# Memory tokens and memory K/V weights ahead of the first modulation weights, their products among them and out of the block attention

## The chip, the core and the metric

The kernel runs on one core of one Trainium2 chip. The metric is the device time of one execution in microseconds, the median of the runs shown. TensorE (PE in the profile) multiplies into eight PSUM banks of 128 x 512 fp32; VectorE (DVE) and ScalarE (ACT) read these and work in SBUF; GpSimd (POOL) builds masks at the start; SyncE (SP) issues nearly all loads, from one queue.

## The reference

Two blocks, one after the other, on 256 tokens of 1024 channels, in fp32. The first computes modulation vectors, a mixer of two halves (a recurrence and causal attention), and a mixture of 32 experts; the second is a stick-breaking attention with an attention on 256 memory tokens, and a feed-forward layer.

```python
# first block
mods = silu(c) @ w_ada + b_ada                      # shift1, scale1, gate1, shift2, scale2, gate2
h = rms_norm(x, norm1_g) * (1 + scale1) + shift1
proj = h @ w_in
y_rwkv = rwkv7_time_mix(proj[..., :RWKV_PROJ], ...)
y_moba = moba_attention(proj[..., RWKV_PROJ:], ...)
x = x + gate1 * (concat(y_rwkv, y_moba) @ w_out)
h = rms_norm(x, norm2_g) * (1 + scale2) + shift2
x = x + gate2 * moe_ffn(h, ...)                     # top 4 of 32 experts
# second block
proj = x @ w_in_sb;  mix = stick_breaking_attention(q, k, v)
mem_out = memory_attention(q_mem, mem, w_mem_kv)    # keys and values: mem @ w_mem_kv
x = layer_norm(ALPHA * x + concat(mix, mem_out) @ w_out, ...)
x = layer_norm(ALPHA * x + square(relu(x @ w_up)) @ w_down, ...)
```

`mem @ w_mem_kv` depends on inputs alone, on nothing that the first block computes. Its result (km, the keys with channels on partitions, and vmem, the values with tokens on partitions) is wanted in the second block only.

## The kernel before

All instructions are written out by hand in one program for each engine; the order in the code is the order on the engine, and semaphores tie the engines. Weights pass through `ring`, ten slots of 2 MB. During the first block's mixer the slots 4 to 7 serve as work space (`ws`), and the slots 0 to 3 take the weights of the prologue, in the order of the list `PRO` (22 entries, `pro_slot(n)`): four pieces of the modulation weights `w_ada` (2 MB each, the first 2048 columns, 256 rows a piece), then the seven pieces of `w_in`, with further pieces of `w_ada` between them, then the memory weights, and the rest. A slot is loaded again when `pro_freed(n)` says that its piece is used, which TensorE counts in `halves_used` and VectorE in `mod_acc`.

**Front.** SyncE loads x, then the first four pieces of `w_ada`. The memory tokens are loaded before entry 4, once the first piece is used. TensorE turns the rows of small parameters (L614, a helper for all transposes), turns x (16 transposes 128 x 128), sums the squares (L628), and multiplies silu(c) with the four pieces (L642, 32 matmuls; a matmul of fp32 gives two records in the profile where its row says so, so that a piece has 8 matmuls and 16 records). The result is copied (L1528), turned, and makes shift and scale; then the memory tokens are turned (four groups, `mem_turned`) and VectorE copies them to `memT` (L1896). ScalarE (L1534) and VectorE (L1892) write the modulated input hT, and the projections start (`proj`, L685).

**Middle.** Projections, the preparation of the recurrence, and the block attention, in which four pairs of heads follow each other (`for i in range(RT)` on PE). Per pair: scores (L758, L759), VectorE adds the position term and takes the maxima (`moba_max`, L2003 to L2009), ScalarE takes exponentials with their sums (`moba_exp`, L1626), VectorE divides (`moba_norm`, L2015 to L2018), TensorE turns the probabilities (6 transposes, L614), issues the scores of the pair after next and one of four parts of the memory product (`mem_kv_part`, L809 for the two halves of km, L812 for those of vmem: 8 matmuls each), ScalarE copies the turned probabilities (L1635, L1636), TensorE multiplies with the values (L851, L853), and ScalarE copies the output (L1640) and, after every second pair, km or vmem from bank 6 (L1643). Then comes the recurrence (`wkv_setup` from L864 on), which waits for the last output copy, the last copy of turned probabilities, and vmem. ScalarE's order in this loop is: copies of pair i, exponentials of pair i + 2, output copy of pair i.

**Experts.** The first loads of expert weights wait for the milestone `y_ready` at the end of the recurrence (the four slots of `ws`), the next for the slots of `w_out`. 32 passes follow, each with six loads of 2 MB, and then the second block.

The waits that the change touches are these:

```python
if n == 4:
    load(mem_tok, a["mem_2"]..., S("mem_in"))          # SP
if job == 1:
    pe.wait_ge(S("memT_ready"), 4)                     # PE, in proj
if i == 2:
    pe.wait_ge(S("mem_kv"), 1)                         # PE, in mem_kv_part
pe.wait_ge(S("mem_kv"), 2)                             # PE, before wkv_setup
```

Of the kernel before, what the change touches and what calls it, by code (L numbers as in the profile page):

```python
# [17 lines left out]
ACT = mybir.ActivationFunctionType  # L18
# [32 lines left out]
N_PRO = 22  # L51
# [54 lines left out]
def build(nc, a, out):  # L106
    ctx = ExitStack()
    with ctx:
# [176 lines left out]
        memT = view(tok_f, 0, [KT, T])  # L285
# [47 lines left out]
        def chunk_cols(w, c0, n):  # L333
# [8 lines left out]
               + [("mem", 0), ("ada", 9), ("out", 0), ("out", 1), ("ada", 10), ("ada", 11)])  # L342
# [14 lines left out]
        def pro_slot(n):  # L357
            return (n + 2) % PRO_RING
# [24 lines left out]
        def _(sp_):  # L383
# [9 lines left out]

            load(tok[:, :, :], a["x"][0].rearrange("(i p) d -> p i d", p=P), S("x_in"))
            for n in range(N_PRO):
# [4 lines left out]
                if n == 4:  # L400
                    load(mem_tok, a["mem_2"][0].rearrange("(i p) d -> p i d", p=P), S("mem_in"))
# [8 lines left out]
                elif kind == "mem":  # L410
                    load(slot8(s), chunk_cols(a["w_mem_kv_2"][0], 0, 512), S(f"pro_in{s}"))
                else:
                    load(slot8(s), chunk_cols(a["w_out"][0], 512 * i, 512), S(f"pro_in{s}"))
# [196 lines left out]
        def _(pe):  # L610
# [7 lines left out]
            tr(B(1)[:, 0:N_FIRST], prow[0:N_FIRST, :], N_FIRST).then_inc(*mark("par_turned"))  # L618
            pe.wait_ge(S("x_in"), 16)
            for b in range(4):  # L620
# [3 lines left out]
                last.then_inc(S("x_turned"), 1)  # L624
            pe.wait_ge(S("xsq_a"), 2)
# [3 lines left out]
            last.then_inc(*mark("xss"))  # L629

# [23 lines left out]
            pe.wait_ge(S("mem_in"), 16)  # L654
            for b in range(4):
                for k in (2 * b, 2 * b + 1):
                    for i in range(TT):
                        last = tr(bank2([7, 0, 2, 3][b])[:, k % 2, i * P:(i + 1) * P], mem_tok[:, i, k * P:(k + 1) * P])
                last.then_inc(S("mem_turned"), 1)

# [8 lines left out]
            def proj(n, job):  # L669
# [3 lines left out]
                for half in range(2):  # L673
# [3 lines left out]
                    if job == 1:  # L677
                        pe.wait_ge(S("memT_ready"), 4)
# [120 lines left out]
            def mem_kv_part(i):  # L799

                if i == 0:
                    arrived(pos("mem", 0))
                    pe.wait_ge(*at("vtok_ready"))
                if i == 2:
                    pe.wait_ge(S("mem_kv"), 1)
                w = slot8(pro_slot(pos("mem", 0)))
                for k in range(KT):
                    if i < 2:
# [5 lines left out]
                if i % 2:  # L814
                    last.then_inc(S("halves_used"), 1)
# [1698 lines left out]
```

## Time and profile before

| what | us |
|---|---|
| median of 3 runs (lowest, highest) | 1549.33 (1546.7, 1549.62) |
| profiled execution, span from first to last instruction | 1549.3 |
| its own time beside the span | none is listed apart from the span |
| PE busy | 1502.3 (97%) |
| PE weight loads | 775.7 (50%) |
| DVE busy | 472.4 (30%) |
| ACT busy | 293.0 (19%) |
| DMA, read from HBM | 501.49 MB, 324 GB/s over the span |

In the profile times are in us from the start of the span. A chain of waits is followed back from the last instruction and shows, piece by piece, what released the next. A timeline row is a merged group of instructions of one line and engine, with the idle time before it and what ended that in brackets. A row of windows gives, for one stretch, the busy time of PE, PE weight loads, DVE, ACT and POOL with their instruction counts, then the granted clock of TensorE as a share of full speed, the busy share of the DMA engines and GB/s.

### The profile page before, as it was taken

The numbers are of one execution on the slowest core, as the hardware profiler recorded it, in microseconds if no ns is written. First come the engines' busy times: TensorE is split into PE (matmuls) and PEld (weight loads), VectorE is DVE, ScalarE is ACT, GpSimd is POOL, SyncE is SP. The second block draws the span as 40 slices with busy tenths as digits, with TensorE's granted clock in tenths as the row PEclk, the third lists the DMA queues.
The fourth block names the chain that finished last, engine by engine and source line by source line (L and its number), as shares of the span: only waits on it lengthen the run. The fifth ranks groups of instructions, "written<-read, shape, count | busy, mean of one in ns | idle before, by whom it ended". The sixth has DMA issues, their size and how long they took to land.

```text
span 1549.3 us, 21348 instructions
## 1 busy us (share of the span) xinstructions
PE 1502.3 (97%) x8793; PEld 775.7 (50%) x8794; DVE 472.4 (30%) x845; ACT 293.0 (19%) x457; POOL 36.9 (2%) x87
## 2 busy tenths in 40 slices
PE   6999899999999999999999999999999999999997
PEld 3875786633333333333333333333333686699643
DVE  2577442412121121211211112111111233466844
ACT  2224312211111111111111111111111233112100
POOL 6000210000000000000000000000000000000000
PEclk9999998999999999999999999999999999999999
DMA  9956104999999999999999999999999933244430
GB/s 373 314 213 243 56 3 195 405 397 429 426 429 428 428 429 429 428 429 429 429 428 429 429 428 430 428 428 429 428 427 428 363 109 109 109 164 164 175 151 27
DMA packets 71972, 503.32 MB, mean 325 GB/s; under 512 B 5278, under 2 KB 8496, under 8 KB 46320
## 3 DMA queue, kind: packets, MB, share of 16 engines
q1 hardware_dynamic: 71026, 500.25, 78.6%
q10 hardware_dynamic: 894, 2.30, 0.4%
q8 instruction: 41, 0.67, 0.2%
q14 instruction: 11, 0.09, 0.0%
HBM read 501.49 MB, written 1.05 MB: 324 GB/s over the span
## 4 chain that ended last, share of the span: by engine, by line
PE 81%; DMA 15%; DVE 2%; ACT 1%; issue 0%; SPq 0%; DVEq 0%
PE psum L1157 21%; DMA ring<-in_w_gate_up 13%; PE psum L1196 12%; PE psum L1458 6%; PE psum L1429 6%; PE psum L685 5%; PE psum L1114 3%; PE psum L1247 3%; PE psum L1098 3%; PE psum L614 3%; PE psum L1189 2%; PE psum L1032 2%; PE psum L1382 2%; DMA ring<-in_w_ada 2%; PE psum L1150 1%; PE psum L732 1%
## 5 line engine op out<-in xcount | busy, mean ns | idle before, releaser
L1157 PE MATMUL psum<-ring,work 128*64 128x512 f32 x2048 | 448.7, 594 | 11.3 <-DMA ring<-in_w_gate_up 11.3
L1157 PEld LDWEIGHTS psum<-ring,work 128*64 128x64 f32 x2048 | 142.6, 137 | 315.2 <-issue 289.2
L1196 PE MATMUL psum<-ring,work 128*64 128x512 f32 x1024 | 226.8, 595 | 0.0
L2235 DVE TENSOR_SCALAR work<-psum 128x512 f32<-128x512 f32 x32 | 22.1, 692 | 451.8 <-PE psum L1157 451.8
L1196 PEld LDWEIGHTS psum<-ring,work 128*64 128x64 f32 x1024 | 70.7, 137 | 153.9 <-issue 153.9
L1730 ACT ACTIVATE work<-work 128x512 f32<-128x512 f32 x32 | 20.1, 629 | 399.4 <-DVE work L2235 399.4
L685 PE MATMUL psum<-ring 128*128 128x256 f32 (+1 forms) x368 | 80.5, 380 | 0.4 <-ACT ring L1534 0.4
L685 PEld LDWEIGHTS psum<-ring 128*128 128x128 f32 (+1 forms) x368 | 68.5, 187 | 13.1 <-issue 2.1
L1114 PE MATMUL psum<-work 64*128 64x256 f32 x528 | 65.9, 389 | 0.7 <-ACT work L1736 0.7
L1736 ACT ACTIVATE work<-psum 128x512 f32<-128x512 f32 x32 | 19.1, 597 | 241.2 <-PE psum L1196 241.2
L1114 PEld LDWEIGHTS psum<-work 64*128 64x128 f32 x528 | 48.3, 186 | 31.9 <-issue 26.0
L1098 PE MATMUL psum<-tok,work 128*64 128x512 f32 x264 | 62.3, 592 | 0.2 <-DVE work L2175 0.2
L1458 PE MATMUL psum<-ring 128*128 128x512 f32 x128 | 59.3, 592 | 0.0
L1247 PE MATMUL psum<-xT,ring 128*128 128x256 f32 x224 | 49.7, 381 | 0.7 <-DVE xT L2255 0.7
L2180 DVE TENSOR_SCALAR work<-ones,id 128x64 f32<-128x64 f32 x33 | 8.4, 254 | 137.7 <-PE psum L1196 137.6
L1716 ACT ACTIVATE mod_acc<-psum 128x512 f32<-128x512 f32 x33 | 35.5, 1077 | 70.0 <-PE psum L1098 70.0
L1247 PEld LDWEIGHTS psum<-xT,ring 128*128 128x128 f32 x224 | 42.1, 190 | 7.6 <-issue 1.8
L1458 PE MATMUL psum<-ring,work 128*128 128x512 f32 x96 | 45.4, 592 | 0.0
L1730 ACT ACT_TABLE_LOAD x32 | 41.1, 1283 | 0.8 <-issue 0.3
L1429 PE MATMUL psum<-xT,ring 128*128 128x128 f32 x336 | 41.0, 275 | 0.0
L1458 PEld LDWEIGHTS psum<-ring 128*128 128x128 f32 x128 | 24.2, 190 | 30.1 <-issue 30.1
L1429 PEld LDWEIGHTS psum<-xT,ring 128*128 128x128 f32 x336 | 39.2, 192 | 0.0
(476 smaller groups left out, 1533.9 us busy)
## 6 DMA issues: line engine op xcount, KB each, us to landing
ring<-in_w_gate_up SPq DMA_DIRECT2D x128, 2048.0 KB, 30.9
ring<-in_w_down SPq DMA_DIRECT2D x72, 2048.0 KB, 28.1
ring<-in_w_ada SPq DMA_DIRECT2D x12, 2048.0 KB, 12.4
ring<-in_w_up SPq DMA_DIRECT2D x8, 2048.0 KB, 7.8
ring<-in_w_in SPq DMA_DIRECT2D x6, 2048.0 KB, 7.9
ring<-in_w_out SPq DMA_DIRECT2D x4, 2048.0 KB, 7.9
ring<-in_w_in_sb SPq DMA_DIRECT2D x4, 2048.0 KB, 20.2
ring<-in_w_mem_kv SPq DMA_DIRECT2D x1, 2048.0 KB, 9.1
```

The lines of the kernel that those rows point to most:

```text
L614: return nc.tensor.transpose(o, i, ident[0:n, 0:n])
L685: last = mm(bank2(bank)[0:m, jj, :], w[:, k, j * P:j * P + m], hT[:, k, :], start=k == 0, stop=k == KT - 1)
L1032: last = mm(bank2(4 + 2 * (n - 18) + half)[:, jj, :], slot8(pro_slot(pos("out", n - 18)))[:, k, j * P:(j + 1) * P], yT[:, k, :], start=k = ...
L1098: last = mm(B(0)[CAP * h:CAP * (h + 1), :], sel[:, ti, :], tok[:, ti, 512 * h:512 * (h + 1)], start=ti == 0, stop=ti == TT - 1)
L1114: last = mm(bank2(4 + m // 2)[:, m % 2, :], ye[CAP * h:CAP * (h + 1), c * P:(c + 1) * P], selT[CAP * h:CAP * (h + 1), :], start=False, sto ...
L1157: ins = mm(B(1 + u)[CAP * h:CAP * (h + 1), :], xe[:, k % 4, k // 4, :], w[:, k % 2, c0:c0 + 512], start=False, stop=k == KT - 1)
L1196: last = mm(B(3)[CAP * h:CAP * (h + 1), :], act[:, k % 4, k // 4, :], w[:, k % 4, 512 * h:512 * (h + 1)], start=False, stop=k == KT - 1)
L1247: last = mm(bank2(b)[:, jj, :], post_w(n)[:, k, c0 + jj * P:c0 + (jj + 1) * P], xT[:, k, :], start=k == 0, stop=k == KT - 1)
L1429: last = mm(o[:, q, :], left[:, k, q * P:(q + 1) * P], right[:, k, :], start=k == 0, stop=k == 3)
L1458: return mm(B(P_BANK[pr]), x, y, start=q == 0, stop=q == 15)
L1716: A(by_four(x_tm), B(0).rearrange("p (q c) -> p q c", c=4), ACT.Copy).then_inc(S("e_xtm"), 1)
L1730: A(sgm, gt, ACT.Sigmoid, scale=1.702).then_inc(S("e_sig"), 1)
```

## The change

SyncE's first two loads are now the memory tokens and the memory weights, into slots of the work space (ring 6 for the tokens as before, ring 7 for the weights `w_kv`); x and the four modulation pieces follow. `memT` moves from `tok` to ring 5. TensorE turns the tokens as soon as they are there, ahead of x, and does the four parts of the product apart: the first ahead of x's turns, the second behind them, third and fourth behind the sum of squares. km stands in bank 2 and vmem in bank 4, and ScalarE copies them there. VectorE's four copies to `memT` come first on its list. The block attention keeps its turns, scores and value products, and the recurrence waits for outputs and copies alone. The list `PRO` loses its entry for the memory weights, and `pro_slot` is rotated by one so that the last entries keep their slots.

```diff
@@ SP
+            load(mem_tok, a["mem_2"][0]..., S("mem_in"))
+            load(w_kv, chunk_cols(a["w_mem_kv_2"][0], 0, 512), S("kv_in"))
             load(tok[:, :, :], a["x"][0]..., S("x_in"))
...
-                if n == 4:
-                    load(mem_tok, a["mem_2"][0]..., S("mem_in"))
-               + [("mem", 0), ("ada", 9), ("out", 0), ("out", 1), ("ada", 10), ("ada", 11)])
+               + [("ada", 9), ("out", 0), ("out", 1), ("ada", 10), ("ada", 11)])
-            return (n + 2) % PRO_RING
+            return (n + 3) % PRO_RING
@@ PE, front
+            pe.wait_ge(S("mem_in"), 16)
+            for b in range(4):
+                if b == 3:
+                    pe.wait_ge(S("memT_ready"), 1)
...
+                last.then_inc(S("mem_turned"), 1)
+            pe.wait_ge(S("kv_in"), 16)
+            pe.wait_ge(S("memT_ready"), 4)
+            mem_kv_part(0)
             pe.wait_ge(S("x_in"), 16)
...
+            mem_kv_part(1).then_inc(S("mem_parts"), 1)
             pe.wait_ge(S("xsq_a"), 2)
...
             last.then_inc(*mark("xss"))
+            mem_kv_part(2)
+            mem_kv_part(3).then_inc(S("mem_parts"), 1)
@@ PE, block attention
-                mem_kv_part(i)
...
-            pe.wait_ge(S("mem_kv"), 2)
@@ ACT
+            ac.wait_ge(S("mem_parts"), 1)
+            A(km[:, :, :], bank2(2), ACT.Copy)
             ac.wait_ge(*at("xss"))
...
+            ac.wait_ge(S("mem_parts"), 2)
+            A(vmem[:, :, :], bank2(4), ACT.Copy)
             ac.wait_ge(S("halves_used"), 8)
...
-                if i % 2:
-                    ac.wait_ge(S("halves_used"), 2 * 11 + i // 2 + 1)
-                    A((km, vmem)[i // 2][:, :, :], bank2(6), ACT.Copy).then_inc(S("mem_kv"), 1)
@@ DVE
+            for b in range(4):
+                ve.wait_ge(S("mem_turned"), b + 1)
+                V.tensor_copy(memT[:, 2 * b:2 * b + 2, :], bank2([2, 3, 0, 2][b])).then_inc(S("memT_ready"), 1)
             for n, b in enumerate((5, 7)):
                 ve.wait_ge(S("x_turned"), b - 3)
```

In the lists below a row is one instruction of TensorE, or several alike (x7), with its line, what it writes and reads, its shape, and the semaphores that it waits for. First the front of the kernel before, from the turns of x (L614, reading tok) over the sum of squares (L628) to the first two modulation pieces (L642):

```order
L614 MATMUL psum<-ident,tok 128x128 [waits x_in]
L614 MATMUL psum<-ident,tok 128x128 x15
L628 MATMUL psum<-ring,ones 128x256 [waits vector_milestones,xsq_a]
L628 MATMUL psum<-ring,ones 128x256 x7
L642 MATMUL psum<-ring,silc_t 32x512 [waits pro_in2,vector_milestones]
L642 MATMUL psum<-ring,silc_t 32x512 x7
L642 MATMUL psum<-ring,silc_t 32x512 [waits pro_in3]
```

The same place of the changed kernel, whose lines are numbered anew (L613 transposes, L630 and L633 the memory product, L650 the sum of squares, L666 the first modulation piece):

```order
L613 MATMUL psum<-ident,ring 128x128 [waits mem_in]
L613 MATMUL psum<-ident,ring 128x128 x11
L613 MATMUL psum<-ident,ring 128x128 [waits memT_ready]
L613 MATMUL psum<-ident,ring 128x128 x3
L630 MATMUL psum<-ring 128x256 [waits memT_ready,kv_in]
L630 MATMUL psum<-ring 128x256 x7
L613 MATMUL psum<-ident,tok 128x128 [waits x_in]
L613 MATMUL psum<-ident,tok 128x128 x15
L630 MATMUL psum<-ring 128x256 x8
L650 MATMUL psum<-ring,ones 128x256 [waits vector_milestones,xsq_a]
L650 MATMUL psum<-ring,ones 128x256 x7
L633 MATMUL psum<-ring 128x256 x16
```

Turns and all four parts of the product stand ahead of the first modulation piece, which in both kernels is the next row.

In the block attention before, on TensorE, the third and fourth pair: turns (L614), a part of the memory product (L812), value products (L851, L853), and the start of the recurrence (L864):

```order
L614 MATMUL psum<-ident,work 128x128 x5
L812 MATMUL psum<-ring,tok 128x256 [waits mem_kv]
L812 MATMUL psum<-ring,tok 128x256 x7
L851 MATMUL psum<-work 64x256 [waits moba_oc,moba_tc]
L853 MATMUL psum<-work 64x128
L851 MATMUL psum<-work 64x256
L853 MATMUL psum<-work 64x128
L614 MATMUL psum<-ident,ring 128x128 [waits moba_p]
L614 MATMUL psum<-ident,ring 128x128 x5
L812 MATMUL psum<-ring,tok 128x256 x8
L851 MATMUL psum<-work 64x256 [waits moba_oc,moba_tc]
```

The same place of the changed kernel (L847, L849 the value products, L860 the recurrence):

```order
L613 MATMUL psum<-ident,work 128x128 x5
L847 MATMUL psum<-work 64x256 [waits moba_oc,moba_tc]
L849 MATMUL psum<-work 64x128
L847 MATMUL psum<-work 64x256
L849 MATMUL psum<-work 64x128
L613 MATMUL psum<-ident,ring 128x128 [waits moba_p]
L613 MATMUL psum<-ident,ring 128x128 x5
L847 MATMUL psum<-work 64x256 [waits moba_oc,moba_tc]
L849 MATMUL psum<-work 64x128
L847 MATMUL psum<-work 64x256
L849 MATMUL psum<-work 64x128
L860 MATMUL psum<-ring 64x64 [waits moba_tc,moba_oc]
```

The value products of a pair now follow its turns directly, and wait for the same copies as before.

## Rows read from the trace of the kernel before

**Rows 1.** The page: granted clock and GB/s in 40 slices of 38.7 us.

```profile
PEclk9999998999999999999999999999999999999999
...
GB/s 373 314 213 243 56 3 195 405 397 429 426 429 428 428 429 429 428 429 429 429 428 429 429 428 430 428 428 429 428 427 428 363 109 109 109 164 164 175 151 27
```

**Rows 2.** Chain of waits, whole run: start us, us, what.

```profile
3.08 23.61 DMA ring<-in_w_ada
26.74 3.42 PE psum L642 x16
...
34.14 38.57 PE psum L685 x176
```

**Rows 3.** Timeline, 0 to 60 us: start, us, engine, line, what [idle before].

```profile
8.33 3.67 PE L614 MATMUL psum<-ident,tok 128*128 128x128 f32 x16
...
14.21 3.69 PE L628 MATMUL psum<-ring,ones 128*128 128x256 f32 x16 [2.21 <-DVE ring L1868]
...
17.83 3.64 PE L642 MATMUL psum<-ring,silc_t 128*32 128x512 f32 x32
...
19.82 0.37 SPq L385 DMA_DIRECT2D ring<-in_mem  x1
...
20.23 4.89 SPq L385 DMA_DIRECT2D ring<-in_w_in  x2
...
26.74 3.36 PE L642 MATMUL psum<-ring,silc_t 128*32 128x512 f32 x16 [3.06 <-DMA ring<-in_w_ada]
...
30.83 2.92 PE L614 MATMUL psum<-ident,ring 128*128 128x128 f32 x22 [0.73 <-ACT ring L1528]
```

**Rows 4.** Load issues: count, KB each, us from issue to landing.

```profile
ring<-in_w_in SPq DMA_DIRECT2D x1, 1152.0 KB, 12.6
tok<-in_x SPq DMA_DIRECT2D x1, 1024.0 KB, 5.0
ring<-in_mem SPq DMA_DIRECT2D x1, 1024.0 KB, 9.4
```

**Rows 5.** Windows of 2 us: PE, PEld, DVE, ACT, POOL busy; clock, DMA, GB/s.

```profile
4.00:6.00 2.00, 0.00 (x0) 0.00 (x0) 0.00 (x0) 0.00 (x0) 1.64 (x7) 1.00 1.04 426
...
26.00:28.00 2.00, 1.26 (x8) 0.40 (x12) 0.00 (x0) 0.00 (x0) 1.60 (x5) 0.57 1.00 395
...
50.00:52.00 2.00, 2.00 (x11) 1.77 (x10) 1.93 (x3) 0.00 (x0) 0.00 (x0) 1.00 1.05 386
```

**Rows 6.** Timeline of the block attention, 120 to 180 us.

```profile
151.65 0.50 ACT L1636 ACTIVATE work<-psum 128x384 f32<-128x384 f32 x1
...
154.68 0.17 DVE L2009 TENSOR_SCALAR small<-small 128x4 f32<-128x4 f32 x1
...
156.20 0.88 PE L614 MATMUL psum<-ident,ring 128*128 128x128 f32 x6
...
156.78 0.18 DVE L2015 RECIPROCAL small<-small 128x4 f32<-128x4 f32 x1 [1.93 <-ACT work L1626]
...
157.50 0.48 ACT L1636 ACTIVATE work<-psum 128x384 f32<-128x384 f32 x1
...
160.09 0.17 DVE L2009 TENSOR_SCALAR small<-small 128x4 f32<-128x4 f32 x1
...
162.74 0.68 DVE L2018 TENSOR_TENSOR ring<-ring,small 128x512 f32<-128x512 f32 x1
```

**Rows 7.** Chain of waits, 125 to 190 us.

```profile
163.38 3.72 PE psum L812 x16
...
172.17 0.59 PE psum L851 x4
172.76 0.25 PE psum L853 x4
...
173.03 0.38 ACT ring L1640
...
174.05 0.35 PE psum L864 x8
```

More of the change, by code:

```diff
@@ L284, in build @@
         mem_tok = view(ws, 9984, [TT, D])
-        memT = view(tok_f, 0, [KT, T])
+        memT = view(ws, 4864, [KT, T])
+        w_kv = ring[:, 7, :].rearrange("p (k n) -> p k n", k=KT)
         ws2 = ring[:, 3:7, :].rearrange("p a b -> p (a b)")
@@ L392, in pro_freed @@
                     sp_.wait_ge(S("halves_used"), halves_before(n + 1))
+            load(mem_tok, a["mem_2"][0].rearrange("(i p) d -> p i d", p=P), S("mem_in"))
+            load(w_kv, chunk_cols(a["w_mem_kv_2"][0], 0, 512), S("kv_in"))
             load(tok[:, :, :], a["x"][0].rearrange("(i p) d -> p i d", p=P), S("x_in"))
@@ L618, in _, with mem_kv_part @@
             tr(B(1)[:, 0:N_FIRST], prow[0:N_FIRST, :], N_FIRST).then_inc(*mark("par_turned"))
+            pe.wait_ge(S("mem_in"), 16)
+            for b in range(4):
+                if b == 3:
+                    pe.wait_ge(S("memT_ready"), 1)
+                for k in (2 * b, 2 * b + 1):
+                    for i in range(TT):
+                        last = tr(bank2([2, 3, 0, 2][b])[:, k % 2, i * P:(i + 1) * P], mem_tok[:, i, k * P:(k + 1) * P])
+                last.then_inc(S("mem_turned"), 1)
+            def mem_kv_part(i):
+                for k in range(KT):
+                    if i < 2:
+                        last = mm(bank2(2)[:, i, :], w_kv[:, k, i * P:(i + 1) * P], memT[:, k, :],
+                                  start=k == 0, stop=k == KT - 1)
+                    else:
+                        last = mm(bank2(4)[:, i - 2, :], memT[:, k, (i - 2) * P:(i - 1) * P], w_kv[:, k, T:2 * T],
+                                  start=k == 0, stop=k == KT - 1)
+                return last
+            pe.wait_ge(S("kv_in"), 16)
+            pe.wait_ge(S("memT_ready"), 4)
+            mem_kv_part(0)
             pe.wait_ge(S("x_in"), 16)
@@ L797, in _ @@
             last.then_inc(*mark("biki_turned"))
[L799 to L808, printed above, removed]
-                        last = mm(bank2(6)[:, i, :], w[:, k, i * P:(i + 1) * P], memT[:, k, :],
-                                  start=k == 0, stop=k == KT - 1)
-                    else:
-                        last = mm(bank2(6)[:, i - 2, :], memT[:, k, (i - 2) * P:(i - 1) * P], w[:, k, T:2 * T],
-                                  start=k == 0, stop=k == KT - 1)
-                if i % 2:
-                    last.then_inc(S("halves_used"), 1)
             def ada_product(x, bank):
@@ L1893, in _ @@
             last.then_inc(S("h_ready_d"), 1)
-            for b in range(4):
-                ve.wait_ge(S("mem_turned"), b + 1)
-                V.tensor_copy(memT[:, 2 * b:2 * b + 2, :], bank2([7, 0, 2, 3][b])).then_inc(S("memT_ready"), 1)
             def mix_chunk(pr, dst, mu0, widths, copied):
```

14 lines of the change are left out of this document (1 added, 13 removed).

## The prediction

> **What bounds the kernel now.** I read the busy and clock rows of the page first [rows 1]: the clock stands at 9 tenths or more in all slices but the seventh, and the DMA moves 373 GB/s in the first slice of 38.7 us, nearly nothing in slices 5 and 6, and then some 428 to the end of the experts. The front of the kernel can thus be bound by loads, the middle can't. The experts' first loads wait for y_ready at the end of the middle, so what the front or the middle gains or loses moves loads and products of the experts together: I carry it to the end one to one.
>
> The chain of waits of the first 60 us [rows 2] then shows the front's end: the load of the fourth modulation piece ends at 26.7, its products run 3.42 us, then come copies and turns, and at 34.14 the first projection starts. From there the chain is TensorE without a gap (38.57 us of L685 in one piece [rows 2]). So the front is worth what the arrival of that fourth piece is worth. The timeline of the front [rows 3] shows that the turns of the memory tokens are done by 33.75 (30.83 + 2.92), before the projection can start at 34.14 behind the modulated input: they cost nothing today. The timeline of the block attention [rows 6] shows the other place: four memory products of about 3.7 us each (one of them stands in [rows 7]), in a row of TensorE work that has hardly a gap.
>
> **The front after the change: loads.** Memory tokens (1.05 MB) and their weights (2.10 MB) go ahead of x and the four pieces. Today the tokens take 26.7 to 29.2 behind the fourth piece (issued 19.82 [rows 3], landed 9.4 later [rows 4]): 2.5 us. The weights have 2 KB rows; where such rows alone are loaded the windows read 386 GB/s, against 426 with the long rows [rows 5], so 2.10 MB are 5.4 us. Together 7.9 us: the fourth piece lands at 34.6. Bounds: everything at 426 GB/s gives 7.4; the weights at the rate of the first projection piece (issued 20.23 [rows 3], landed 12.6 later [rows 4]: 1.18 MB from 29.2 to 32.8, 328 GB/s) give 8.9. I take 7.9, since the 386 comes from the same shape.
> The Trainium skill ("DMA: Bandwidth & Descriptors", section "Where 436 GB/s comes from") says that reads from HBM are held to about 358 GB/s for a core and that only the fabric reaches 435. The windows here show 426 from HBM, so the measurement decides; by the page the step would be 8.8 us and not 7.9.
>
> **The front: TensorE.** Can it still be ready when the fourth piece lands? The turns start at 8.33 as now, since they wait for the small rows as well [rows 3]. 16 turns 3.67, VectorE's fourth copy 0.69 behind them: memT at 12.9. First product 1.85 (half of the 3.72 for 16 records) to 14.7; x lands at 5.8 + 5.4 + 2.5 = 13.7; its turns 3.67 to 18.4; second product to 20.2, beside VectorE's copy and squares, which today end 2.2 us after the last turn: 20.6. Sum of squares 3.69 to 24.3, third and fourth product 3.7 to 28.0, first and second modulation piece 3.64 to 31.6, third 1.82 to 33.4. That is 1.2 us ahead of the fourth piece, so of the four products nothing stands on the path: they fill waits for loads. If TensorE were late by more than 1.2, each us beyond it would count.
> The front's cover: the first projection piece can be issued when the first modulation piece is used (about 29.8), ahead of 34.6, and lands 3.6 behind it, at 38.2; it is wanted at 40.5. The second has to be there 24 matmuls of 0.44 us later (38.57 over 176 records, two to a matmul), 10.5 us, and follows in 5.4. So no new wait, but only 2.3 us of cover. SyncE passes nothing else: its later loads wait for the same slots, and one fewer is among them.
> One thing is given back. Today TensorE stands idle 3 us before the fourth piece, its clock falls to 0.57 of full speed (the lower of its levels, 1.2 GHz, for most of that stretch), and 16 records take 3.36 us; the first 32 took 3.64, so 16 take 1.82 at full clock [rows 3, 5]. With a wait of 1.2 in place of 3 I expect full clock: -1.5. The front costs 7.9 - 1.5 = **+6.4** (5.9 to 8.9).
>
> **The block attention after the change.** 64 matmul records, four times 3.7 = 14.8 us, leave TensorE, but they cover a ring of VectorE and ScalarE. I replay it with the durations of [rows 6]. Probabilities are copied out by ScalarE at 152.15; the first value product (0.84, [rows 7]) ends at 153.0, second turns (0.88) and scores (some 0.9) at 154.8. ScalarE copies the second pair only after its third exponentials, which end at 156.75 because VectorE's scores and maxima end at 154.85: copies to 158.0, as today. VectorE and ScalarE go on as they do now: norm to 158.0, scores and maxima to 160.26, exponentials to 162.15, copy of the second output to 162.5, copies of the third pair to 163.4, last norm to 163.4. TensorE: second values 158.85, third turns 159.7, then it waits for 163.4. From there the chain is bare: third values 164.3, fourth turns 165.15, two copies 166.1, fourth values 167.0, output copy 0.38, start of the recurrence at 167.5. Today it starts at 174.05, behind the copy of vmem [rows 7]. Gain **-6.5**, not 14.8: 8.3 us of the products were cover. Bounds: 0 if ScalarE's chain should stretch by what it no longer waits for, 14.8 if all were bare; the replay has every duration from a row, and I take it.
>
> **The clock.** Both edits leave gaps. In the block attention TensorE has 8.3 us of work in 17.4, with idle stretches of 3.2 and 3.7 us. In the front, behind the fourth piece, the turns of the memory tokens no longer fill 31.9 to 33.8, so that TensorE stands 2.3 us before the first projection. What the trace shows of such places: after 3 us idle at 26.7 the clock is 0.57 [rows 5], and the seventh slice, with its small products and short gaps, stands at 8 tenths [rows 1]. A fall doubles what is on the path. In the block attention that is third values, fourth turns, fourth values (2.5 us) and the first two groups of the recurrence, some 1 us each (up to 2); in the front about 1.5 at the start of the projection, which is what the spell at 26.7 took (3.36 - 1.82). Bounds 0 and 6.0. I take 0.9 for the front and 2.0 for the block attention: a fall is likely at each, full length is not.
> The Trainium skill ("TensorE: Matmul & The Clock Gate", "Part 4: PE-mode transpose") says that transposes don't count as activity for the gate as matmuls do. No row here separates them. By it the block attention, which is left with turns for much of its work, would fall to 1.2 GHz almost surely, and the sum would take the full 4.5 there and not 2.0.
>
> **Sum.** +6.4 + 0.9 - 6.5 + 2.0 = +2.8 us. The profiled execution spans 1549.3 us, the median of the three runs is 1549.33, nothing else lies around it: **1552 us**, rounded. Below I call within 0.2% (3.1 us) no change, which is about what a measurement of this kernel can tell.
> At nothing: the two ScalarE copies of km and vmem lie beside TensorE's products in the front, and VectorE's four copies are in the steps above. Rotating the slots and the freed slot in the middle: every wait for a load is already hidden there.
>
> **Rivals.** (A) The forecast, loss and gain cancel: 0.46.
> (B) Slower: the clock falls in the block attention and stays down into the recurrence, and also at the first projection. For it: idle stretches longer than the one at 24 to 26.7. Against it: the gap of 2.2 us before 14.21 [rows 3] was followed by products at full clock. Price 2.5 + 2 + 1.5 = 6.0: 7.9 - 1.5 - 6.5 + 6.0 = +5.9, 1555.2; with the slow products of the fourth piece too, 1556.7. It decides from a clock loss of 3.2 us on. 0.41.
> (C) Faster: the replay is too strict and the four products were bare. For it: the chain of waits names all four as path, and it goes on from their end [rows 7]. Against it: ScalarE's exponentials wait for VectorE's maxima at 154.85 and 160.26 today [rows 6], with or without the products. 6.4 - 14.8 = -8.4, 1540.9; half of it, 1545. 0.10.
> (D) It doesn't do what it says: TensorE is not ready at 34.6, because the weights land late or the turns wait, so that two products (3.7) stand ahead of the fourth piece: 2.5 beyond the margin, 1554.6. 0.03.
>
> Range: (A) alone 1549 to 1553.5; to hold eight in ten it needs most of (B) and the edge of (C): 1548 to 1557. Faster 0.10, same 0.46, slower 0.44.
>
> **What would show it.** Fourth modulation piece landed near 34.6 with its 16 records in about 1.9 us; first projection at 40.5 to 41.5; no DMA wait in front of the projections; recurrence starting 6.5 minus clock loss earlier against the first projection than today (139.9 us between them now, 133.4 or a little more after); clock row under 1.0 in the block attention. Wrong if the distance stays near 139.9, if it falls under 130, or if the projection starts before 39 or after 43.

## The result and the profile after

| kernel | median, us | lowest to highest | runs |
|---|---|---|---|
| before | 1548.27 | 1546.7 to 1549.62 | 4 |
| after | 1559.84 | 1558.92 to 1561.87 | 4 |

The ratio on record is 1.0072, with a 95% interval of 1.0057 to 1.0088 (it is not formed from the two medians, whose quotient is 1.0075): slower by some 11 us, and 7.8 us above the forecast of 1552, outside its range of 1548 to 1557. The profiled execution of after took 1559.4 us; its span is 1557.6, so 1.8 us lie around the span. Between the two traces the span grew by 8.3. One of the ten executions of e3 below took 1944 us and is left out of its median, as a slow one.

Page of after, the same rows as [rows 1]:

```profile
PEclk9999798899999999999999999999999999999999
...
GB/s 363 290 268 218 53 3 137 408 382 429 427 427 429 427 430 428 427 429 429 428 429 428 429 428 429 429 428 429 428 427 428 377 109 108 108 163 163 167 157 27
```

The clock row has two weak places where before had one: the fifth slice (7 tenths, 155.8 to 194.7 us, the block attention and the first groups of the recurrence), besides the seventh and eighth. The experts' part reads 427 to 430 GB/s as before, and the waits of the experts for their loads are 11.5 us against 11.3: what the front and the middle lose or gain is carried to the end, as forecast.

Chain of waits of after from 0 to 45 us, the same view as [rows 2]:

```profile
1.32 10.82 DMA ring<-in_w_mem_kv
...
12.18 3.72 PE psum L630 x16
15.90 1.75 PE psum L613 x16
17.64 3.46 PE psum L630 x16
21.10 3.45 PE psum L650 x16
24.55 6.91 PE psum L633 x32
31.46 7.05 PE psum L666 x64
...
40.38 2.08 ACT ring L1533 x4
...
42.50 2.50 PE psum L700 x5
```

L630 is the first and the second part of the product, L633 the third and fourth, L650 the sum of squares, L666 the four modulation pieces. There is no wait for a modulation piece any more: from 12.2 to 38.5 TensorE is the chain. A part takes 3.46 us at full speed, 16 turns 1.75. The projection starts at 42.50, 8.36 later than before [rows 2].

Windows of after, as in [rows 5]: the early loads, the wait ahead of the projection, and the block attention into the recurrence.

```profile
4.00:6.00 2.00, 0.00 (x0) 0.00 (x0) 0.00 (x0) 0.00 (x0) 1.64 (x7) 1.00 0.94 363
6.00:8.00 2.00, 0.86 (x4) 0.77 (x5) 0.00 (x0) 0.00 (x0) 1.24 (x7) 1.00 1.01 332
8.00:10.00 2.00, 2.00 (x11) 2.00 (x10) 1.27 (x2) 1.11 (x1) 1.59 (x7) 1.00 1.06 404
...
42.00:44.00 2.00, 1.50 (x4) 1.23 (x5) 0.00 (x0) 0.45 (x1) 0.00 (x0) 0.50 1.07 368
...
166.00:182.00 16.00, 12.21 (x132) 9.04 (x132) 5.34 (x13) 5.72 (x19) 1.77 (x1) 0.50 0.01 2
```

TensorE was idle for 2.3 us ahead of 42.5 and began the projection at half speed (1.2 GHz); its 176 records took 39.99 us instead of 38.57. From 166 to 182 it ran at half speed throughout. It had been idle for 3.07 us in front of the first of these rows of its timeline:

```profile
165.92 1.13 PE L847 MATMUL psum<-work 128*64 128x256 f32 x4 [3.07 <-ACT work L1635]
...
171.28 1.13 PE L847 MATMUL psum<-work 128*64 128x256 f32 x4 [2.33 <-ACT work L1635]
...
172.76 1.54 PE L613 MATMUL psum<-ident,ring 128*128 128x128 f32 x6
```

The value products took 1.13 us where they had 0.66 in the timeline of before (next row), the turns 1.54 where they had 0.88 [rows 6]. The recurrence starts at 177.32 against 174.05 [rows 7].

```profile
172.10 0.66 PE L851 MATMUL psum<-work 128*64 128x256 f32 x4
```

Then something that the prediction does not have. GpSimd does not only build masks at the start of the kernel; it also takes vector steps of the recurrence. The first steps of VectorE (first fence) and of GpSimd (second fence) there, in after:

```profile
184.17 1.69 DVE L2047 TENSOR_TENSOR ring<-work,ring 128x512 f32<-128x512 f32 x1
...
187.17 1.75 DVE L2054 TENSOR_TENSOR ring<-ring 128x512 f32<-128x512 f32 x1
```

```profile
184.04 1.27 POOL L604 TENSOR_TENSOR work<-work,ring 128x512 f32<-128x512 f32 x1 [2.15 <-ACT work L1647]
186.63 1.74 POOL L604 TENSOR_TENSOR work<-work,ring 128x512 f32<-128x512 f32 x1 [1.32 <-PE psum L899]
```

and the same steps of VectorE before:

```profile
180.04 0.67 DVE L2051 TENSOR_TENSOR ring<-work,ring 128x512 f32<-128x512 f32 x1
...
182.02 0.69 DVE L2058 TENSOR_TENSOR ring<-ring 128x512 f32<-128x512 f32 x1
```

A step with two operands in SBUF takes 0.67 us alone, and 1.69 when a GpSimd step began 0.13 us ahead of it (1.75 in place of 0.69 for the second, where GpSimd began 0.54 ahead): 2.08 us in two places, on the path. Before, GpSimd's steps at this place fell beside VectorE's steps that read PSUM. I call this the meeting of VectorE and GpSimd.

Adding up along the two traces: projection start +8.36; its clock +1.42; a half-speed spell at 94 to 98 us that the first trace of before has and after hasn't, -1.66; block attention -4.82 (from the first turns, 150.07 and 158.16, to the recurrence). That is +3.27 at the start of the recurrence. Its first groups at half speed and the meeting of VectorE and GpSimd add 2.95, so that it ends 6.22 later (213.93 and 220.15). The last 2.1 us up to 8.3 arise behind the recurrence, where half-speed spells stand in both traces at slightly different places; they are not followed up one by one. The spell in the chain of before:

```profile
94.43 1.87 PE psum L723 x2
96.30 1.71 PE psum L724 x2
```

The same four records take 1.06 and 0.86 us in after.

### The profile page after: what moved, and what is told of

The parts are those of the page before. It is cut to its first block, busy times and chain, and to the rows that moved or that the text cites. A ratio compares the mean times of both kernels' runs of the same rounds, so it can differ in the third digit from the quotient of the medians.

```text
span 1557.6 us, 21348 instructions
## 1 busy us (share of the span) xinstructions
PE 1507.2 (97%) x8793; PEld 781.7 (50%) x8794; DVE 475.6 (31%) x845; ACT 293.6 (19%) x457; POOL 37.8 (2%) x87
## 4 chain that ended last, share of the span: by engine, by line
PE 82%; DMA 14%; DVE 3%; ACT 1%; issue 0%; SPq 0%; DVEq 0%
PE psum L1152 21%; DMA ring<-in_w_gate_up 13%; PE psum L1191 12%; PE psum L1453 6%; PE psum L1424 6%; PE psum L700 5%; PE psum L1109 3%; PE psum L1242 3%; PE psum L613 3%; PE psum L1093 3%; PE psum L1184 2%; PE psum L1027 2%; PE psum L1377 2%; PE psum L1145 1%; PE psum L747 1%; PE psum L1392 1%
## 5 line engine op out<-in xcount | busy, mean ns | idle before, releaser
L1152 PE MATMUL psum<-ring,work 128*64 128x512 f32 x2048 | 448.8, 594 | 11.5 <-DMA ring<-in_w_gate_up 11.5
```

The costliest lines, as they stand in the source:

```text
L1152: ins = mm(B(1 + u)[CAP * h:CAP * (h + 1), :], xe[:, k % 4, k // 4, :], w[:, k % 2, c0:c0 + 512], start=False, stop=k == KT - 1)
```

## The experiments

The ratio of each run is to executions of before that were measured beside it, whose median was 1548.4 to 1549.7; after itself was measured earlier, beside 1548.27, so a difference of medians to its 1559.84 is good to 2 us or so. A point to compare traces by is the first copy of the recurrence (ScalarE's L1651 of before): 175.25 us before, 179.38 after. The 175.25 holds the spell of 1.66 at 94 to 98; the second trace of before (e12), without it, has 174.35.

| run | median, us | ratio to before, 95% interval | projection start | first copy |
|---|---|---|---|---|
| e1_no_products | 1558.02 | 1.0063 (1.0043 to 1.0084) | 44.03 | 180.59 |
| e2_eighth_of_weights | 1560.39 | 1.0063 (1.0041 to 1.0085) | 44.23 | 182.68 |
| e3_block_alone | 1545.47 | 0.9975 (0.9960 to 0.9990) | 34.10 | 168.46 |
| e4_block_clock | 1554.77 | 1.0032 (1.0019 to 1.0046) | 44.63 | 180.13 |
| e5_warm_gap | 1556.17 | 1.0046 (1.0030 to 1.0061) | 44.61 | 180.16 |
| e6_fourth_part_late | 1554.50 | 1.0034 (1.0021 to 1.0047) | 43.05 | 178.47 |
| e10_pieces_alone | 1559.24 | 1.0060 (1.0040 to 1.0080) | 43.55 | 181.93 |
| e11_both_fills | 1551.15 | 1.0009 (0.9998 to 1.0020) | 43.51 | 176.08 |
| e7_half_front | 1550.81 | 1.0015 (1.0002 to 1.0028) | 38.88 | 173.34 |
| e8_warm_products | 1547.21 | 0.9999 (0.9987 to 1.0012) | 34.80 | 174.22 |
| e9_spread_products | 1548.85 | 0.9999 (0.9986 to 1.0013) | 33.69 | 173.15 |
| e12_before_again | 1549.14 | 1.0002 (0.9989 to 1.0014) | 35.20 | 174.35 |

### The front: loads without products, products without loads

e1_no_products:

```diff
-            mem_kv_part(0)
-            mem_kv_part(1).then_inc(S("mem_parts"), 1)
+            pe.sem_inc(S("mem_parts"), 1)
-            mem_kv_part(2)
-            mem_kv_part(3).then_inc(S("mem_parts"), 1)
+            pe.sem_inc(S("mem_parts"), 1)
```

> The changed kernel without the four parts of the memory product (km and vmem are left out of the computation; loads, turns and copies stay). Theory T, TensorE is the bound of the front: each part is 3.5 us there (6.9 for two), so without them TensorE is ready early, the fourth modulation piece (landed about 33.9) decides, and the first projection starts near 39.7 instead of 42.5; the span falls by about 2.8 us. Rival L, the loads ahead of x are the whole cost: the start stays at 42.5 and the span with it.

Theory T fails: with no product at all the front is no faster. Its chain of waits:

```profile
7.19 28.52 DMA ring<-in_w_ada
...
35.75 3.69 PE psum L664 x16
...
44.03 40.68 PE psum L698 x176
```

The fourth piece lands at 35.71, 1.1 later than in my sum, and after an idle time of 3.8 us its 16 records run at half speed, 3.69 us. With the loads and what the wait for them does to the clock, the start is 44.03.

e2_eighth_of_weights:

```diff
-            load(w_kv, chunk_cols(a["w_mem_kv_2"][0], 0, 512), S("kv_in"))
+            load(w_kv[:, 0, :], a["w_mem_kv_2"][0][0:P, 0:512], S("kv_in"))
-   ... w_kv[:, k, ...]
+   ... w_kv[:, 0, ...]
```

> The changed kernel with only the first 128 rows of the memory weights loaded (256 KB instead of 2 MB) and used for every part, so the same matmuls on wrong values. Theory T: TensorE is busy from 12.0 on with products, turns, squares and modulation and ends at 38.2 as before; first projection near 42.2, span at most 0.5 us less. Rival L: 1.84 MB less ahead of the pieces bring the projection start to 38, span about 4.5 us less.

With an eighth of the weights to load the start is as late again, so rival L fails too:

```profile
11.70 5.94 PE psum L630 x16
...
26.29 6.91 PE psum L633 x32
33.20 7.05 PE psum L666 x64
...
44.23 2.07 PE psum L700 x4
```

TensorE alone brings 44.2. So two bounds stand at the same place, and taking either one away gives nothing. The four parts stand in the chain with 5.94 + 3.46 + 6.91 us. Here the first part took 5.94 where after's profile has 3.72: TensorE's first work runs at half speed, and the moment when it comes up differs by execution. In the other four traces with this first part (e4, e5, e6, e11) it took 5.2 to 6.0 us as well, so the start of 42.50 in after's trace is the lucky one.

e10_pieces_alone asks why the piece lands late (e1 and this):

```diff
+                if n == 4:
+                    sp_.wait_ge(S(f"pro_in{pro_slot(3)}"), 16)
```

> The kernel without the four product parts (the memory K/V product is left out, its loads stay), and SyncE holds the first load of the projections' pieces until the fourth modulation piece has landed. Without the hold that piece landed at 35.71 us in this kernel, 1.1 later than the sum had it. Theory S (transfers queued behind it took part of the engines' time): it lands at 34.3 to 34.8, and the projection starts about 1 us earlier, at 43; the pieces of the projections land later than before but before they are wanted. Time 1557 to 1558.5. Rival (the rate was just lower): it lands at 35.5 to 36 all the same and the projection waits for its first piece, time 1558 or more.

Theory S fails, and the rival has the landing right (35.9). Windows of this run at the end of the fourth piece:

```profile
33.00:33.50 0.50, 0.00 (x0) 0.00 (x0) 0.00 (x0) 0.00 (x0) 0.00 (x0) 1.00 0.95 393
33.50:34.00 0.50, 0.00 (x0) 0.00 (x0) 0.00 (x0) 0.00 (x0) 0.00 (x0) 1.00 0.66 246
34.00:34.50 0.50, 0.00 (x0) 0.00 (x0) 0.00 (x0) 0.00 (x0) 0.00 (x0) 1.00 0.08 33
```

The bulk of the bytes has moved by 33.9, and two last rows of 8 KB (the 33 GB/s of the third window) by 34.5, but TensorE is released at 35.9: the landing is seen 1.4 us behind the last bytes. In e1, with other loads behind it, the landing is at 35.71, no later. So no cost of the loads queued behind it is seen.

Part of the lateness is the rate of the first microseconds: 363 and 332 GB/s from 4 to 8 us in after, against 426 [rows 5] and 420 before, and 404 against 428 in the window behind them, which is 0.35 MB or 0.8 us. All bytes at 426 GB/s would have landed 7.4 us behind 26.7, and the landing is 9.0 behind it; so this is half of the difference of 1.6, of which the prediction's 7.9 had allowed 0.5. Where the other half lies is open. Before's windows:

```profile
6.00:8.00 2.00, 0.00 (x0) 0.00 (x0) 0.00 (x0) 0.00 (x0) 1.24 (x7) 1.00 1.01 420
8.00:10.00 2.00, 1.93 (x9) 1.85 (x10) 0.00 (x0) 1.47 (x2) 1.59 (x7) 1.00 1.04 428
```

### The block attention

e3_block_alone, the kernel before without the products there:

```diff
-                mem_kv_part(i)
+                if i == 0:
+                    arrived(pos("mem", 0))
+                if i % 2:
+                    pe.sem_inc(S("halves_used"), 1)
...
-            pe.wait_ge(S("mem_kv"), 2)
```

> The kernel before with the four products taken out of the block attention and nothing put in the front (loads and turns stay; km and vmem get other contents). My replay: recurrence starts at 167.5 if the clock stays full, 6.5 us earlier than 174.05. With the clock falling as in the changed kernel: 169.2 (4.8 earlier), its first groups 0.9 slower, and up to 2.1 lost where VectorE and GpSimd meet: span 1544.5 to 1546.5 against 1549.3. Rival C, the products were bare: 14.8 earlier.

The four parts of the product are gone, and the first copy of the recurrence stands at 168.46, 6.8 earlier. Of this 1.7 are not the edit's: the spell at 94 to 98 is missing here, so the block attention starts that much earlier. From the second pair's exponentials, which begin at 147.80 here and at 149.53 before, to the recurrence (166.40 and 174.05) it is 18.6 us against 24.5, 5.9 less. The whole kernel gains 4.2 (1545.47 against 1549.7), and rival C, with 14.8, is refuted. The last value products are at half speed here too, as the chain of waits of e3 shows:

```profile
164.35 1.13 PE psum L854 x4
```

e4_block_clock, after with fillers, that is, matmuls whose results nobody reads, in the waits:

```diff
+            def fill(n):
+                for j in range(n):
+                    mm(bank2(6)[:, j % 2, :], ones[:, :], qk[:, j % 8, :], start=True, stop=True)
+            pe.wait_ge(*at("vtok_ready"))
+            fill(3)
...
+                fill([0, 6, 7, 2][i])
```

> The changed kernel with 18 idle-time matmuls of 128x256 (results unused) in the waits of the block attention: 3 ahead of the first turns, 6, 7 and 2 in the waits of pairs two to four. Theory T: the clock stays at full speed, the recurrence starts 1.7 us earlier (175.6), its first groups take 0.9 less, and if the meeting of VectorE and GpSimd at 184 to 189 follows from that delay another 2.1 come back: span 2.6 to 4.7 us less. Rival: the clock isn't the reason, the fillers cost up to 1 us.

Work that nobody needs makes the kernel 5 us faster (1554.77 against 1559.84). The front of this trace is 2.1 us later than in after's, and yet the first copy is 0.75 later only, and the end of the recurrence earlier (218.82 against 220.15). From the second pair's exponentials (161.39 and 157.76) to the recurrence's end it is 57.4 us against 62.4. The clock reads 1.00 in all windows from 158 to 182, and VectorE does not meet GpSimd:

```profile
184.93 0.68 DVE L2055 TENSOR_TENSOR ring<-work,ring 128x512 f32<-128x512 f32 x1
```

```profile
183.56 1.37 POOL L604 TENSOR_TENSOR work<-work,ring 128x512 f32<-128x512 f32 x1 [0.90 <-ACT work L1655]
```

The first row is VectorE's timeline, the second GpSimd's: at full speed ScalarE's copy releases GpSimd sooner against VectorE, and its step ends at 184.93, just when VectorE's begins.

Yet the full meeting is in after's trace alone. In e1, e2, e3, e6 and e10 the clock fell to 0.50 in the block attention too, and the same step of VectorE took 0.83 to 0.97 us and the second one 0.69. The two steps in the chain of waits of e2, where a step counts only from what released it:

```profile
187.54 0.77 DVE ring L2047
...
189.71 0.60 DVE ring L2054
```

In the chain of after they stand with 1.61 and 1.67:

```profile
184.25 1.61 DVE ring L2047
...
187.25 1.67 DVE ring L2054
```

What differs is how long the half speed lasts beyond the first copy of the recurrence: up to 182 in after, 2.6 us behind the copy at 179.38, but only 0.8 to 1.1 us beyond that copy in the other five. So the slow clock is needed for the meeting but does not bring it by itself. In e2 and e10, whose block attention is that of after, the same stretch is 60.4 us: against them the fillers of e4 give back 3.0 us, and only against after's own trace 5.0. After's profiled execution had the lucky start and the unlucky meeting, about 2 us each, and e2's has neither.

### The clock at the projection, and TensorE's list

e5_warm_gap:

```diff
+            for j in range(5):
+                mm(bank2(6)[:, j % 2, :], ones[:, :], xT[:, j, :], start=True, stop=True)
```

> The kernel after, with five filler matmuls (128x256, ten records, results unused) on TensorE between the last turns of the memory tokens and the first projection, where the engine stood idle 2 us. Nothing of the computation is left out. Theory C (the clock fell because the engine stood idle ahead of the projection): the first projection's 176 records take 38.6 us instead of 39.99, the start stays within 0.5 us of 42.5 for a front like the profiled one of after, and the time falls by 1 to 2 us, to about 1558. Rival (the clock fell because the products before were too thin, or the drop was luck): the records take 40 to 41.6 us as in after and the time is after's.

The clock's part is confirmed: 38.51 us instead of 39.99 (41.5 in e2 and e4, which start as unluckily as this one). The median falls by 3.7, more than the 1 to 2 expected; against e2 and e4 the projection gives 3.0. The edit also has TensorE wait for the copies of x (`xcopy_a`, `xcopy_d`) ahead of the modulation pieces, so that the fillers may read them.

```profile
42.25 2.36 PE psum L709 x10
44.61 38.51 PE psum L702 x176
```

e6_fourth_part_late:

```diff
-            mem_kv_part(3).then_inc(S("mem_parts"), 1)
...
+                if n == 3:
+                    mem_kv_part(3, range(4))
...
+            mem_kv_part(3, [4])
...
+            mem_kv_part(3, [5, 6, 7]).then_inc(S("mem_parts"), 1)
```

> The kernel after, with its fourth product part (3.5 us) cut up: four matmul groups ahead of the wait for the fourth modulation piece, one after it, three in the gap ahead of the first projection. Nothing is left out. Theory T (TensorE is what ends last in the front: each part costs 3.5 to 3.7 us and not 1.85): about 2 to 3 us of work go into waits, the projection starts at 40 to 41 instead of 42.5 for the same start clock, its records take 38.6 us since the gap is filled, and the time falls by 3 to 4 us, to 1555.5 to 1557. Rival L (the fourth piece lands at about 35.7 whatever TensorE does, and the steps behind it set the start): start at 42 to 44, only the clock's 1.4 us come back, time about 1558.

1554.5, 5.3 under after. The projection started at 43.05, with a first part of 5.23; e5, with 5.67, started at 44.61, and had its weights 0.3 earlier, so the cut itself gave about 1.4, where 2 to 3 had been expected. The rest goes with the filled gap: the first projection took 38.57 us here. The chain shows why the cut gave little: four matmuls ahead of the last piece end at 37.16, still behind a landing at 35.7 to 35.9 (e1, e10).

```profile
29.95 5.29 PE psum L667 x48
35.24 1.92 PE psum L633 x8
37.16 1.90 PE psum L667 x16
```

e11_both_fills is e6 with the fillers of e4.

```diff
 (e6)
+            fill(3)
...
+                fill([0, 6, 7, 2][i])
```

> The kernel after, with the fourth product part cut up as in the run that moves it into waits, and with 18 filler matmuls (results unused) in the waits of the block attention. Nothing is left out. Theory: the two gains add. The cut part gives 3 to 4 us and the fillers gave 5 (1554.8 against 1559.8), so the time is 1551 to 1553, the recurrence starts about 17.5 us behind the first exponentials and VectorE's first vector steps don't meet GpSimd's. Rival (the front is bound by arrival and the gains don't add): 1554 to 1556.

1551.15: the gains add for the greater part (5.3 and 5.1 alone, 8.7 together, with intervals of some 2 us on each). This is near the forecast of 1552, reached with the clock held up in the two places where it fell, and even so it is not faster than before. Its clock reads 1.00 in every window from 158 to 182 us. It is also the test of the replay of the block attention at full speed: from the first turns (157.82 in e11's timeline) to the recurrence (174.85) it took 17.0 us, where the replay has 17.4 (150.07 to 167.5) and before took 24.0.

### Candidates to beat both kernels

e7_half_front puts the tokens and the key half in front and leaves the value half where it was.

```diff
+            load(mem_tok, ..., S("mem_in"))
+            load(w_k, chunk_cols(a["w_mem_kv_2"][0], 0, T), S("mem_in"))
...
+            for i in range(2):       # keys, behind the sum of squares
+                for k in range(KT):
+                    last = mm(bank2(2)[:, i, :], w_k[:, k, i * P:(i + 1) * P], memT[:, k, :],
...
-                mem_kv_part(i)
+                if i in (1, 2):
+                    mem_kv_part(i - 1)
```

> A kernel between the two: the memory tokens and the key half of the memory weights (1 MB instead of 2) load ahead of the modulation weights, and two product parts run there; the value half stays in its place among the projections' pieces, and its two parts stay in the block attention. Nothing is left out. Theory: the front costs the tokens' and the half's transfer, 1.5 MB or about 4 us, and TensorE's two parts and turns fit in waits: projection start at 38 to 40 (34.1 before, 42.5 after); the block attention gets back 3 to 5. Time 1548 to 1553. Rival (the loads in front cost nothing as long as TensorE has room): start at 35 to 36 and 1545 or less.

```profile
32.92 1.97 PE psum L657 x16
...
38.88 40.21 PE psum L691 x176
```

Here the piece lands at 32.9, 6.2 later than before for 2.1 MB, and TensorE is ready for it, at full speed. The front costs 4.7, its clock 1.6, and the first copy is at 173.34, 1.9 earlier than in the first trace of before and 1.0 earlier than in e12. The median is 1550.81 all the same, 1.7 above before (ratio 1.0002 to 1.0028). The recurrence itself takes 0.8 us longer than in both traces of before, with the clock at 0.50 from 180 to 182, so that e7 is only 0.2 ahead of e12 at its end; the trace shows no more of the 1.7.

e8_warm_products and e9_spread_products stay with the kernel before.

```diff
+                if n == 3:
+                    for j in range(6):
+                        mm(bank2(6)[:, j % 2, :], ones[:, :], xT[:, j, :], start=True, stop=True)
```

> The kernel before, with six filler matmuls (128x256, results unused) on TensorE while it waits for the fourth modulation piece. Nothing is left out. Theory C (the engine's clock is down when the piece lands, since it stood idle for 4 us): the piece's 16 records take 1.8 us instead of 3.36, the projection starts 1.5 us earlier, and the time is 1546.5 to 1548.5 against a before of 1549.7. Rival (the fillers are too thin to hold the clock up): no change.

```profile
26.06 2.86 PE L641 MATMUL psum<-xT,ones 128*128 128x256 f32 x12
28.85 1.92 PE L647 MATMUL psum<-ring,silc_t 128*32 128x512 f32 x16
```

The piece's products do run at full speed, 1.92 us, but the fillers end 2.1 us behind 26.8, where the piece lands in the two traces of before, since the sum of squares took 6.51 us in this execution instead of 3.69. No difference shows in the time (0.9987 to 1.0012).

```diff
 (e8)
+            mem_kv_some(3)          # ahead of the first pair
...
-                mem_kv_part(i)
+                mem_kv_some([6, 7, 8, 8][i])
-                        last = mm(bank2(6)[:, i - 2, :], memT...   # values
+                        last = mm(bank2(1)[:, i - 2, :], memT...
```

> The kernel before with the same six fillers, and the 32 matmul groups of the memory K/V product spread over five waits of the block attention as 3, 6, 7, 8 and 8 instead of four times 8, the first three ahead of the first pair. Nothing is left out. Theory: the fillers give 1.5 and the spread takes up to half of the 4 us that the products cost there (without them the kernel took 1545.7): 1545.5 to 1548, faster than both kernels. Rival (the products' time in the block attention does not depend on where they stand, since the chain of exponentials and turns waits for all of them): 1548, no gain beyond the fillers.

The first copy is 1.1 us earlier than in e8, which is what the start of the projection is earlier (33.69 and 34.80), so the trace shows no gain from the spread, as the rival has it; nor does the time, at 0.9986 to 1.0013. Neither beats before.

e12_before_again is the kernel before without an edit. It is to find the 2 us between the 8.3 of the two spans and the 10.7 by which after's median stands over the 1549.1 of before in most of these measurements.

> The kernel before, unchanged, to see how much of its profile differs from one execution to the next. The two traces compared so far differ by 8.3 us of span, the medians by 10.7. Theory V (the first trace of the kernel before was a slower one): a time of 1546 to 1549 with a span 1.8 below it, and the missing 2 us at places where the first trace has the low clock: the two half-clock products at 94.4 to 98 (1.8 us) or those at 240 to 252. Rival (the start differs): the sum of squares takes 5 to 6.5 us for its 16 records, as it did in two other kernels, instead of 3.69, and the first projection starts at 35 to 37, since TensorE is then the one that ends last.

```profile
26.89 2.94 PE psum L642 x16
...
30.50 4.70 PE psum L614 x22
35.20 38.30 PE psum L685 x176
```

This profiled execution took 1552.76 us with a span of 1551.0, the longest of its ten (1545.57 to 1552.76). The spell at 94 to 98 is missing and the projection starts 1.1 later than in the first trace, because the turns ran at half speed (4.70 us against 2.92 [rows 3]). Theory V fails, since this execution is slower and not faster. The rival has the start right, and the sum of squares too (5.18 us), but not the reason: TensorE still waited 2.0 us for the fourth piece. Half-speed spells move from one execution to the next. Why both profiled executions of before are among its slower ones stays open, and with it about 2 of the 10.7 us.

## Why the prediction was wrong

**The steps that failed** are two: the price of the products in the front, and the clock in the block attention, which was put at 2.0. By the two traces the sum, in us, compares like this:

| term | predicted | measured |
|---|---|---|
| start of the projection | +6.4 | +8.36 |
| its clock | +0.9 | +1.42 |
| block attention with its clock, up to the end of the recurrence | -6.5 + 2.0 | -4.82 + 2.95 |
| spells that the sum has not | 0 | -1.66 + 2.1 |
| in all | +2.8 | +8.3 |

**The products in the front.** The step is "First product 1.85 (half of the 3.72 for 16 records)". A part of the product is 8 matmuls, that is 16 records, as the chain says x16 in [rows 7]; I halved it. The same prediction has 3.7 for a part in the block attention and 0.44 for a matmul of the projection, and either would have shown the slip. A part costs 3.46 us, four cost 13.8 and not 7.4. The turns of x, at full speed, gave 1.9 of that back (1.75 where the sum has 3.67), and other terms 1.2, so TensorE was ready for the fourth piece at 36.7 instead of 33.4. The margin of 1.2 us became an overrun of 2.1 over the 34.6 of the forecast. That is the outcome of rival (D), with 0.03, but not for its reasons: neither late weights nor turns that wait, but the price of a part. In the executions with a slower first part it is some 2 us more.

**The loads.** The piece was to land at 34.6 and landed at 35.7 to 35.9 (e1, e10), 9.0 to 9.2 behind 26.7 and so just outside my bounds of 7.4 to 8.9. With the slow products behind it (3.69 us), this would have been enough alone: e1 started at 44.03. The two errors stand side by side, not one behind the other. Nor do they explain the whole miss: the projection started 2.0 us later than forecast, and 1552 + 2 would still be inside the range.

**The refund** of -1.5 for the fourth piece's clock came true in after (7.05 us for 64 records, 1.76 for 16), where TensorE no longer waited. Where it did wait (e1, e10), the piece cost 3.65 to 3.69.

**The block attention.** The replay gave -6.5 at full speed, and this part of the prediction was right. e11, at full speed, measured -6.9 from the first turns to the recurrence, e3 -5.9 with part of it at half speed, and after's own rows follow the replay to the start of the third value products. Rival (C), products all bare, is refuted.

**The clock** was the right risk, mis-sized: 0.9 put and 1.4 (up to 3.0) found at the projection; 2.0 put for the block attention, where e4's fillers got back 5.0 against after's trace and 3.0 against e2 and e10. The half speed went on through the first groups of the recurrence and in after's trace moved GpSimd's steps onto VectorE's. For that second effect I had no term; it cost 2.1 us in this one trace and 0.2 to 0.3 in five others. Rival (B) had the mechanism, at 1555.2. With the overrun of 2.1 on top it makes +8.0, which is the 8.3 between the spans; it stays 3 us short of the medians.

The Trainium skill ("TensorE: Matmul & The Clock Gate", "Part 4: PE-mode transpose") says that a transpose doesn't count as PE-busy the way a matmul does. By it the prediction would have taken the full 4.5 for the block attention, which is nearer to the 3.0 to 5.0 found than the 2.0 that it took. The fall came (0.50 from 166 to 182); that matmuls put into the waits prevented it (e4) fits the page, but would also fit the plain idle time, so no run here separates the two.

**The reckoning around the span.** I took nothing beside it; every execution with both numbers shows 1.7 to 1.8 us. That is in both kernels and in no difference, but it hid that before's first trace is an execution of about 1551 (1549.3 + 1.8).

## What to carry to other kernels

Price work that is moved in the records of its own row: 13.8 us of products found room in the front only because their own loads had pushed the last landing back by 9 us, so taking away either the loads or the products gave nothing. Look for the second bound before paying to remove the first. And where work leaves TensorE, look at what stands behind the gap: the block attention fell to half speed once the products had left it, and 18 matmuls that nobody reads, put into its waits, gave back 3 to 5 us; but six put ahead of a landing overran it. Last, an effect found in one trace, like the meeting of VectorE and GpSimd, has to be looked for in the others before it goes into the account.

## What the runs showed of the hardware

- The granted clock is listed as 1.00 for the first microseconds, yet TensorE's first work runs at the pace of half speed: 5.94 us in e2 for 16 records that take 3.46 later, 3.67 us before for 16 turns that take 1.75 in after. In after's trace the 16 records took 3.72, so the end of the slow start varies by some 2 us from one execution to the next. The Trainium skill ("TensorE: Matmul & The Clock Gate", "What's actually happening") says that the throttled state is the default and that activity releases it; the durations agree, the listed clock does not.
- VectorE's step on two SBUF operands took 1.69 us instead of 0.67 beside a GpSimd step that began first, and ended 0.55 us behind it, as if it had waited and then run. The Trainium skill ("SBUF — State Buffer", "Who interferes with whom") says that an instruction of VectorE with two SBUF inputs contends with one of GpSimd that reads SBUF, that the shared ports are an exclusive lock, and that the order of issue decides who blocks; the trace agrees, and steps that read PSUM (1.28 us for two) were not slowed. In e2, where GpSimd's step began 0.95 us ahead and had 0.31 left to run, VectorE's took 0.85 and ended 0.54 behind it.
- A load's landing was seen 1.4 us after its last bytes (e10), and it came no later with other loads queued behind it (35.71 in e1, 35.9 in e10; one execution each).
- From 4 to 8 us, loads moved 332 to 363 GB/s in after, where the memory tokens and then the memory weights with their 2 KB rows are first in line, and 420 to 426 before, with x and the long rows of the modulation weights. That the row length is the cause is not shown.
